# A two-layer decoder trunk: another rule for which engine takes an expert's V row

## What is computed

```python
s = jnp.einsum('thpd,hpkd->thpk', q, sub_keys)
sv, si = lax.top_k(s, PEER_TOPK)
cand = sv[:, :, 0, :, None] + sv[:, :, 1, None, :]
top, pos = lax.top_k(cand, PEER_TOPK)
eidx = jnp.take_along_axis(cidx, pos, axis=-1)
g = jax.nn.softmax(top, axis=-1)
a = jnp.einsum('thkd,td->thk', u_tab[eidx], xc)
w = (g * jax.nn.gelu(a)).astype(xc.dtype)
return jnp.einsum('thk,thkd->td', w, v_tab[eidx])
```

## Time and profile before

| | |
|---|---|
| median of 3 runs | 2994.68 us |
| profiled execution, its time | 2995.3 us |
| its span in the trace | 2993.5 us |
| TensorE matmul busy | 2658.8 us (89%) |
| VectorE busy | 2049.6 us (68%) |
| ScalarE busy | 1486.5 us (50%) |
| GpSimd busy | 1170.5 us (39%) |
| moved by DMA | 1198.55 MB, 400 GB/s over the span |
| VectorE multiply-adds of V rows (line 1550) | 45 |

### The profile page before, as it was taken

One profiled execution on the slowest core, in us unless ns is written; L12 is line 12 of the kernel. 1 busy time (PEld: TensorE's weight loads), 2 busy tenths in 40 slices (PEclk: granted clock), 3 DMA queues, 4 the chain that ended last, 5 costly groups with the idle time before them and its releaser, 6 DMA issues.

```text
span 2993.5 us, 29340 instructions
## 1 busy us (share of the span) xinstructions
PE 2658.8 (89%) x8492; PEld 1469.1 (49%) x8492; DVE 2049.6 (68%) x5035; ACT 1486.5 (50%) x4089; POOL 1170.5 (39%) x1028
## 2 busy tenths in 40 slices
PE   8988888999899789999899998989999988777777
PEld 7753455745565345554455553754455543222222
DVE  3478687687699964566557888677657888644444
ACT  3247444387355543447534555458734555433333
POOL 0234422245344443434434344334434444434342
PEclk9999999999999999999999999999999999999999
DMA  6699998899999999999999999999999999999997
GB/s 230 246 401 404 418 380 339 311 420 421 421 421 414 398 416 421 421 421 421 421 422 421 420 418 420 394 421 413 421 421 421 421 409 421 411 421 422 422 421 330
DMA packets 167342, 1198.55 MB, mean 400 GB/s; under 512 B 19856, under 2 KB 20112, under 8 KB 22160
## 3 DMA queue, kind: packets, MB, share of 16 engines
q0 software_dynamic: 147456, 1073.81, 86.9%
q1 hardware_dynamic: 19728, 122.86, 10.2%
HBM read 1194.50 MB, written 2.10 MB: 400 GB/s over the span
## 4 chain that ended last, share of the span: by engine, by line
PE 43%; DMA 36%; DVE 11%; ACT 6%; issue 3%; POOL 1%; DVEq 0%; ACTq 0%; SPq 0%; POOLq 0%
DMA ring<-in_uv,idx 34%; PE psY L1265 25%; PE psP L1138 7%; PE psP L1145 5%; DVE ring L1539 4%; PE psP L1142 2%; ACT L909 1%; ACT L1100 1%; ACT ring L1109 1%; POOL ring L886 1%; PE psT L1123 1%; ACT wgt L1105 1%; DMA wr<-in_w_out 1%; DMA wr<-in_w_in 1%; PE psS L1173 1%
## 5 line engine op out<-in xcount | busy, mean ns | idle before, releaser
L1265 PE MATMUL psY<-ring 128*128 128x512 f32 x3916 | 1845.8, 614 | 281.5 <-ACT ring L1109 278.3
L886 POOL DMA_INDIRECT ring<-in_uv,idx x1024 | 1170.3, 1143 | 1794.0 <-PE psY L1265 1570.7
L1539 DVE CUSTOM_DVE_ANT_0 ring<-ring,htok 128x1024 f32<-128x1024 f32 x1024 | 1238.4, 1222 | 685.9 <-DMA ring<-in_uv,idx 680.2
L1265 PEld LDWEIGHTS psY<-ring 128*128 128x128 f32 x3916 | 729.7, 195 | 1236.8 <-issue 1229.5
L1100 ACT ACTIVATE gl<-adot 128x1 f32<-128x1 f32 x1024 | 204.3, 200 | 1006.9 <-DVE adot L1539 1004.2
L1109 ACT ACTIVATE ring<-cst,wgt 128x128 f32<-128x128 f32 x979 | 393.1, 402 | 31.9
L1105 ACT ACTIVATE wgt<-gate,gl 128x1 f32<-128x1 f32 x1024 | 301.7, 295 | 33.2
L1138 PE MATMUL psP<-hT,wr 128*128 128x256 f32 (+1 forms) x1632 | 308.0, 345 | 6.9 <-DMA wr<-in_w_q 5.3
L1138 PEld LDWEIGHTS psP<-hT,wr 128*128 128x128 f32 x1632 | 269.3, 193 | 53.2 <-issue 18.3
L1145 PE MATMUL psP<-wr,hT 128*128 128x256 f32 x1152 | 257.9, 379 | 0.2 <-DMA wr<-in_w_in 0.2
L1145 PEld LDWEIGHTS psP<-wr,hT 128*128 128x128 f32 x1152 | 218.5, 190 | 52.5 <-issue 22.6
(11 more groups left out here) (145 smaller groups left out, 1521.7 us busy)
## 6 DMA issues: line engine op xcount, KB each, us to landing
wr<-in_w_q SPq DMA_DIRECT2D x40, 1024.0 KB, 9.1
wr<-in_w_in SPq DMA_DIRECT2D x34, 1024.0 KB, 9.1
wr<-in_w_out SPq DMA_DIRECT2D x17, 1024.0 KB, 9.4
ring<-in_uv,idx POOLq DMA_INDIRECT x1024, 18.4
ring<-in_w_in SPq DMA_DIRECT2D x10, 1024.0 KB, 16.5
probs<-in_subkeys SPq DMA_DIRECT2D x5, 1024.0 KB, 17.0
ring<-in_w_out SPq DMA_DIRECT2D x3, 1024.0 KB, 4.8
cat<-in_g_ffn SPq DMA_DIRECT2D x5, 512.0 KB, 12.4
```

Of the source, the lines that this page charges most:

```text
L886: pool.indirect_dma_start(out=ring[:, q % NR], out_offset=None, in_=tables[s // NC], in_offset=bass.IndirectOffsetOnAxis(ap=idx[:, s % NS, ...
L1265: last = nc.tensor.matmul(psY[:, b * 512:(b + 1) * 512], ring[:, r % NR, 0:P], ring[:, r % NR, D + b * 512:D + (b + 1) * 512], start=first ...
L1539: v.tensor_tensor_reduce(out=u, in0=u, in1=htok[:, q // SLOTS % NS], scale=1.0, scalar=0.0, op0=ALU.mult, op1=ALU.add, accum_out=adot[:, J ...
```

## The change

The rule for who adds a row loses one condition and has another loosened. Before, a row went to VectorE when three or more rows stood in TensorE's list, none stood in VectorE's, and the next row had not landed. After, it goes there when three or more stand in TensorE's list and at most one in VectorE's, whether or not the next row has landed.

```diff
         elif key[0] == "r":
             state["r"] += 1
-            by[key[1]] = int(len(rows["pe"]) >= PE_ROWS and len(rows["dve"]) == 0 and state["u"] not in landed)
+            by[key[1]] = int(len(rows["pe"]) >= PE_ROWS and len(rows["dve"]) <= 1)
             rows["dve" if by[key[1]] else "pe"].append(key[1])
             us = 0.7 if by[key[1]] else 1.0
```

## The result

The changed kernel takes 3011.65 us (median of 4 runs, 3009.31 to 3013.67) against 2993.8 us for the kernel before in the same comparison (4 runs): ratio 1.006, 95% interval 1.0042 to 1.0077. In a later comparison (after_again, 5 runs) it took 3006.37 against 2993.67 us, ratio 1.0046 (1.0033 to 1.0059). So the change costs 13 to 18 us, about half a per cent, where 6.5 us of gain were forecast, and the time is above the range: rival A's side, though, as will be seen, not rival A's mechanism.

What follows compares the result with a forecast made beforehand. The bound was taken to be the DMA transfer of 1198.55 MB at 421 GB/s. Terms -9 - 2.5 + 6 - 1 = -6.5 us gave 2988.8, and 2988.2 us as median of the runs; range for 8 in 10: 2975 to 3002.

Steps and rivals of the forecast that it cites:

- rival A: Searches at 925 to 1075 us: VectorE is the bound, its V rows and clumps cost +13 to +17; 3005 us, chance 0.12.
- everywhere else: Stretches outside the four priced ones: DMA is at 421 GB/s and a moved V row hides behind it; no change.
- Projection of steps 2 and 3: 500 to 600 us before: one longer wait, then gathers cover the later pieces; 15 to 20 us lost, not 28.7; -9 us.
- The cross-check: Projection's eleven pieces: 82 to 87 us of DMA work in 102 us, so 15 to 20 us lost instead of 28.7.
- Rival C: Projection's hole only moves, or the searches give the gain back: -2 to +4 us, taken as 2995 us; chance 0.26.
- 400 to 600 up to 358 GB/s: Sign: bandwidth from 400 to 600 us rises from 334 to about 358 GB/s.
- Searches of step 1: 400 to 500 us: one lost gather (+2.5) against some 5 us gained; -2.5 us, from -6 to +4.
- Searches of steps 2 and 3: 785 to 1075 us: VectorE gets twelve more V rows and falls behind; +6 us, bounds 2 and 13.
- VectorE over 140 us busy: Sign for 925 to 1075 us, stated together with a bandwidth of 380 to 395 GB/s.
- the balance of work per eight rows: Searches of steps 2 and 3: 19.9 us of DMA against 21.5 of VectorE work, 1.6 us behind, 2.9 with a V row.
- Input of steps 6 and 7: 1775 to 2050 us: 15 VectorE rows instead of 13 in step 4, in longer runs; -1 us, from -4 to +4.
- Rival D: V rows on VectorE lengthen gather issues beside them, 0.94 to 1.97 us at most: 21 us, 3015 us; chance 0.02.

Runs made afterwards that it cites:

- after_again: The changed kernel measured once more, unaltered, against the kernel before: +12.7 us, ratio 1.0046 (1.0033 to 1.0059).
- clumped: Kernel before, with VectorE's dot products between step 2's and step 3's searches put behind the second for six heads; against the kernel before +12.6 us, 1.0048.
- spread: Kernel before, with a dot product put between search parts standing end to end in steps 2 and 3; against the kernel before +2.1 us, 1.0011.

## Why the prediction was wrong, point by point

**Which steps failed.** Three terms of the sum, by what the parts measured alone. Up to row 212: -9 and -2.5 forecast, -1.2 measured. Rows 212 to 319: +6 forecast, +12.6 measured, by another cause. From row 320 on: -1 and "everywhere else" 0 forecast, +5.5 measured. The last is a term that was put at nothing without the order of that stretch having been compared.

**What bounds the kernel: right.** The loss could be placed by the bandwidth of each stretch, and so could that of every experiment.

**Projection of steps 2 and 3: mechanism right, sum incomplete.** A single wait of about 40 us (44.12), then nine gathers without one over 5 us (the next long ones, 7.66 and 10.24, are shorter than the 14.91 and 14.10 of before), the first half worse and the second better: all as worked out. Row 144 is asked for 8.5 us sooner (12.8 to 16.0 in the four other executions). The second half lost 3.2 us, as worked out (0 to 3); the first lost 23.5 (223 GB/s), so that the two together lost 26.8 where 15 to 20 were forecast. The cross-check was short as well: it gave the eleven pieces 102 us with "some 7 for transposes and scores", and they took 119.1 (499.5 to 618.6 us; 112.4 and 114.8 in two other executions), because parts of the mixer stand between pieces 7 and 8 and between 9 and 10 in the new order. Above all the bill behind 600 us was missing. The pieces 8 to 10 of the new order come 19 to 29 us later by the trace (piece 10 at 618.6 us, before at 590.0), V row 135 stands behind pieces 8 and 9, and row 145 cannot be fetched before it:

```profile
605.10 0.94 POOL L886 DMA_INDIRECT ring<-in_uv,idx  x1 [11.91 <-PE psY L1265]
```

From 600 to 785 us 5.3 to 7.9 us are lost in the kernels with these orders. No run moved the late pieces alone, so that they make this whole loss is argued from the trace. The step that failed is that a stretch's gain was booked at the stretch's end. Rival C (0.26) had this part right ("What the second half wins the longer run loses"): alone, the part measured -1.2 us. The sign "400 to 600 up to 358 GB/s" was missed as well, with 338 (369 and 308), and 348 (373 and 324) in the kernel with only rows below 212.

**Searches of step 1: -2.5 forecast, -0.2.** Within its bounds.

**Searches of steps 2 and 3: sign right, cause wrong, size short.** +6 from 2 to 13 was forecast, mostly from the V rows' own 9.0 us; +9.3 by bandwidth, and +12.6 as a whole in the kernel with only these rows changed, inside the bounds by luck, since the terms that gave them were others. The sign "VectorE over 140 us busy" came true (142.17), but it is no sign of the cause: 144.24 us busy gave 399 GB/s; 377 GB/s is just under the 380 to 395. The V rows, moved alone, cost +0.4 (interval about -2.4 to +3). The clumps, which stood in one sentence of the prediction with no term of their own, cost 12.6 when made by hand. The wrong step is the balance of work per eight rows: it asks whether VectorE has enough time, when the question is how long it goes without a dot product. The ring has ten slots, 24.9 us of DMA. A row needs its way from issue to landing, its dot product, its weight and its V row before the slot is free. My reading, which no run measured piece by piece: a 15 us hole in the dot products leaves too little for the rest, and the burst of eight dot products behind it cannot give the DMA time back. Rival A ended on the right side and at a near price, by the mechanism that the runs refute.

**Input of steps 6 and 7: -1 forecast, -3.3.** Within its bounds.

**Everywhere else 0: wrong, and as large a miss as any.** "A moved V row hides behind it" is true, and beside the point: between rows 376 and 454 no V row is on VectorE in either kernel, but the parts of the mixer of steps 4 and 5 stand otherwise, so that the first search of step 4 comes six rows later. 8.7 us by bandwidth, 6.4 and 5.5 us by the runs. The row that would have warned is the 8.32 us wait for the index at 1605.38 before the change: there was little slack at that place, and the order of that stretch was the thing to compare. Why the planner comes out six rows later there was not settled; the parts differ by at most two rows between 320 and 403 and by -16 to +9 rows behind that.

**Rival D: no sign.** GpSimd's mean issue went from 1143 to 1128 ns with twenty more V rows on VectorE, and it is 1131 ns (clumped) and 1150 ns (spread) with the same 45 as before, so the V rows leave no mark on it. The Trainium skill (SBUF — State Buffer, "Who interferes with whom") speaks of a GpSimd instruction that reads SBUF; whether the issue of a gather is one no run here shows, so the rival went further than that sentence does.

## What to carry to other kernels

Here a ring that is filled in order was starved by the longest holes in the work that empties it, not by that engine's busy share: look in the order for parts that now stand end to end, and price the hole. When a rule feeds a planner, the change is the whole new order and not the rows that the rule names; compare where the first work of each later group stands, above all where the profile already shows a wait for it. A gain at one place is real only if the queue is still ahead at the next place that can lose it.

## What the runs showed of the hardware

Eleven V rows more on VectorE, 14 us of its time, from 785 to 1075 us, where it was 86 and 91% busy before, made no difference that could be measured (+0.4 us). TensorE's granted clock in 925 to 1075 us was 0.93 before, 0.86 with the eleven rows moved and 0.83 in the changed kernel. The figure is a mean of stretches at the 2.4 and at the 1.2 GHz level, and in these three it is the lower, the less TensorE was busy (123.72, 112.56 and 108.09 us). The loss does not go with it: 399 GB/s at 0.86 and 374 at 0.88 (clumped).
